# The first expert's input rows are picked by a one-hot product out of SBUF instead of being gathered from DRAM, with the overflow plan and the next index list moved in among its products

## The reference, cut to what matters

```python
def hier_moe(h, p):
    ...
    combine = jnp.einsum('nk,nke->ne', w2, jax.nn.one_hot(eid, N_EXPERTS, dtype=jnp.float32))
    for e in range(N_EXPERTS):
        he = jax.nn.silu(tok @ p['w_exp_gate'][e]) * (tok @ p['w_exp_up'][e])
        y = y + combine[:, e:e + 1] * (he @ p['w_exp_down'][e]).astype(jnp.float32)
```

## Time and profile before

| | |
|---|---|
| median of 3 runs | 1083.66 us (1080.24 to 1084.55) |
| profiled execution, its own time | 1078.97 us |
| its span, first to last instruction | 1077.1 us |
| TensorE busy | 86% of the span |
| DMA, mean over the span | 273 GB/s |
| DMA, 600 to 620 us | 424 GB/s |

### The profile page before, as it was taken

How to read it: one execution, slowest core, us unless ns; L and a number is a source line. 1 busy time by engine, 2 the same in 40 slices (tenths; PEclk the granted TensorE clock), 3 DMA queues, 4 the chain that set the end, 5 groups by cost and what they waited for, 6 DMA issues and landing times.

```text
span 1077.1 us, 14439 instructions
## 1 busy us (share of the span) xinstructions
PE 930.1 (86%) x5814; PEld 625.3 (58%) x5826; DVE 365.8 (34%) x754; ACT 321.5 (30%) x504; POOL 329.3 (31%) x276
## 2 busy tenths in 40 slices
PE   3788999998998989999988999999988888889840
PEld 3677989896897978988653443344333333333310
DVE  4300145845231213858951221212221212112118
ACT  1473343342786858634221000000000000001102
POOL 7544467772234233552010111111111111112112
PEclk9998999999899999999989999999999999999975
DMA  9825534456467692367486999999999999999831
GB/s 325 257 79 103 114 97 78 103 133 169 154 183 216 175 266 101 128 241 290 184 367 249 407 424 425 426 425 426 424 425 427 426 425 426 426 423 425 349 145 56
DMA packets 60821, 294.13 MB, mean 273 GB/s; under 512 B 7525, under 2 KB 9165, under 8 KB 48162
## 3 DMA queue, kind: packets, MB, share of 16 engines
q1 hardware_dynamic: 49296, 272.68, 68.6%
q0 software_dynamic: 6560, 11.47, 3.1%
q10 hardware_dynamic: 4914, 9.28, 2.4%
HBM read 290.23 MB, written 14.68 MB: 283 GB/s over the span
## 4 chain that ended last, share of the span: by engine, by line
PE 46%; DMA 35%; DVE 9%; ACT 5%; issue 4%; POOL 1%; SPq 0%; POOLq 0%; ACTq 0%
DMA ring<-in_w_exp_up 21%; PE bank L1428 13%; DMA ring<-in_w_in 7%; PE bank L1080 5%; PE bank L1451 5%; PE bank L1082 5%; PE bank L1081 5%; DMA cond_slot<-in_w_cond 2%; PE bank L1031 1%; DMA ring<-in_w_branch_a 1%; DMA expert_inputs<-hf 1%; DMA ring<-in_w_cond 1%; PE bank L1418 1%; DVE hf L1941 1%; PE bank L1136 1%
## 5 line engine op out<-in xcount | busy, mean ns | idle before, releaser
L538 POOL TENSOR_TENSOR w_lo<-ring,w_hi 128x1024 fp32r<-128x1024 f32 x80 | 191.9, 2413 | 197.2 <-ACT w_hi L757 197.2
L1428 PE MATMUL bank<-ring,hf 128*64 128x512 f32 x1024 | 229.5, 601 | 17.9 <-DMA ring<-in_w_exp_up 17.0
L1080 PE MATMUL bank<-h_hi,w_hi 128*128 128x320 f32 x576 | 186.1, 323 | 18.0 <-POOL w_lo L538 7.9
L1082 PE MATMUL bank<-h_hi,w_lo 128*128 128x320 f32 x576 | 181.0, 314 | 0.0
L1428 PEld LDWEIGHTS bank<-ring,hf 128*64 128x64 f32 x1024 | 79.6, 139 | 164.3 <-issue 156.4
L1451 PE MATMUL bank<-ring,he 128*64 128x512 f32 x512 | 129.9, 654 | 0.7 <-DVE he L1945 0.5
L1080 PEld LDWEIGHTS bank<-h_hi,w_hi 128*128 128x128 f32 x576 | 111.1, 193 | 23.5 <-ACT va L698 5.4
L1081 PE MATMUL bank<-h_lo,w_hi 128*128 128x320 f32 x384 | 120.4, 314 | 0.0
L1082 PEld LDWEIGHTS bank<-h_hi,w_lo 128*128 128x128 f32 x576 | 110.9, 192 | 0.0
L594 POOL DMA_INDIRECT xrow<-expert_inputs,sidx x32 | 32.8, 1024 | 250.8 <-DVE sidx L1931 230.8
L1941 DVE TENSOR_TENSOR hf<-hf,bank 64x512 f32<-64x512 f32 x32 | 22.1, 690 | 230.2 <-ACT hf L939 230.2
(11 more groups left out here) (376 smaller groups left out, 1276.8 us busy)
## 6 DMA issues: line engine op xcount, KB each, us to landing
ring<-in_w_exp_up SPq DMA_DIRECT2D x32, 2048.0 KB, 34.2
ring<-in_w_exp_down SPq DMA_DIRECT2D x32, 2048.0 KB, 33.5
ring<-in_w_exp_gate SPq DMA_DIRECT2D x32, 2048.0 KB, 29.5
ring<-in_w_in SPq DMA_DIRECT2D x16, 2048.0 KB, 14.0
cond_slot<-in_w_cond SPq DMA_DIRECT2D x9, 2048.0 KB, 11.7
ring<-in_w_cond SPq DMA_DIRECT2D x3, 2048.0 KB, 17.7
ring<-in_w_branch_b SPq DMA_DIRECT2D x2, 2048.0 KB, 7.9
ring<-in_w_branch_a SPq DMA_DIRECT2D x2, 2048.0 KB, 10.8
```

What stands on the lines that cost most here:

```text
L538: pool.tensor_tensor(w_lo[slot][:, :, c], raw[:, :, c], w_hi[:, :, c].bitcast(F32), ALU.subtract)\
L1080: mm(b, hi[:, k, c], x_hi[:, k, :], start=(k == 0), stop=False)
L1082: last = mm(b, lo[:, k, c], x_hi[:, k, :], start=False, stop=(k == KT - 1))
L1428: last = mm(bank[1][64 * q:64 * q + 64, :], xg[:, k % 4, k // 4, :], ring[s + q][:, k * FF:k * FF + FF], start=(k == 0), stop=(k == KT - 1 ...
```

## The change

Expert 0 no longer takes its rows from DRAM. `first_rows` multiplies the token rows in `hf` (stationary, 128 of every fourth column at a time) with the first 64 columns of `onehot` (moving): for each of 2 halves `c` and 4 quarters `q`, three matmuls over the token tiles. VectorE copies the halves out of banks 2 and 0 into `xg_first`, which lies in `gf_rows`; the hidden rows of expert 0 lie there too (`gs_first`). The gather of expert 0 goes, and so do the 16 idle products and the four transposes ahead of `gate_up(0)`. `gate_up(0)` is cut in two halves, with `index(1)` and one product of the plan between them; the other three products of the plan and `index(2)` follow it. On ScalarE `silu(0)` and `rows_out(0)` now stand ahead of the wait for `hf_out`. On VectorE the end of the plan and `one_hots(2)` stand ahead of `gated(0)`.

```diff
+        xg_first = gf_rows[:, 0, 0:CB].rearrange("p (q c s) -> p q c s", q=4, c=2)
+        gs_first = gf_rows[:, 0, CB:CB + FF]
...
             pool.wait_ge(S["hf_out"], 48)
-            gather(0, 0, 0, False)
             gather(1, 1, 1, False)
...
+            silu(0, gs_first)
+            rows_out(0, 0, None)
             act.wait_ge(S["hf_out"], 48)
-            for e in range(3):
+            for e in range(1, 3):
                 step(e, e, None)
...
+            def first_rows():
+
+                pe.wait_ge(S["hb_ready"], 6)
+                pe.wait_ge(S["onehot_ready"], 1)
+                for c, (b, done) in enumerate(((bank[2], "xg_half"), (bank[0], "xg_t"))):
+                    for q in range(4):
+                        for t in range(3):
+                            m = TR[t]
+                            last = mm(b[:, q * SLOTS:(q + 1) * SLOTS], hf[0:m, t, c * CB + q:c * CB + CB:4],
+                                      onehot[0:m, t, 0:SLOTS], start=(t == 0), stop=(t == 2))
+                    last.then_inc(S[done], 1)
...
             idle_products(bank[3], 4)
+            first_rows()
             index(0)
...
-            index(1)
-            pe.wait_ge(S["flag_ready"], 1)
-            mm(bank[4][:, 0:1], tri_strict[:, :], flags[:, 0:1], start=True, stop=True).then_inc(S["xr_ps"], 1)
...
+            pe.wait_ge(S["half_ready"], 1)
+            gate_up(0, 0, use_0, xg_first, range(KT // 2))
+            index(1)
+            pe.wait_ge(S["flag_ready"], 1)
+            mm(bank[4][:, 0:1], tri_strict[:, :], flags[:, 0:1], start=True, stop=True).then_inc(S["xr_ps"], 1)
+            gate_up(0, 0, use_0, xg_first, range(KT // 2, KT))
             pe.wait_ge(S["pick_ready"], 1)
...
-            idle_products(bank[3], 16)
-            turn_rows(0, 0, 16)
-            step(0, 0, lambda s: expert_use(s, 0), 1, 16)
+            index(2)
+            turn_hidden(0, gs_first)
+            turn_rows(1, 1, 16)
+            down(0, 0, use_0)
...
+            dve.wait_ge(S["xg_half"], 1)
+            V.tensor_copy(xg_first[:, :, 0, :], bank[2][:, 0:4 * SLOTS].rearrange("p (q s) -> p q s", q=4))\
+                .then_inc(S["half_ready"], 1)
+            dve.wait_ge(S["xg_t"], 1)
+            V.tensor_copy(xg_first[:, :, 1, :], bank[0][:, 0:4 * SLOTS].rearrange("p (q s) -> p q s", q=4))\
+                .then_inc(S["xg_ready"], 1)
             indexed(0, 0)
...
-            gathered(0)
-            step(0, 2)
+            one_hots(2, 2, None)
+            gated(0, gs_first)
+            indexed(2, 2)
+            turned(0)
+            gathered(1)
```

More of the change, by code:

```diff
@@ L323, in build @@
             flag_ready xr_ps pick_ready plan_ps plan_ready gfr_in gfr_ps gf_ready onehot_ready
-            xg_t xg_ready gu_ps gs_ready hrow_ready he_t he_ready down_ps ys_ready scattered0
+            xg_half half_ready xg_t xg_ready gu_ps gs_ready hrow_ready he_t he_ready down_ps ys_ready scattered0
             scattered1 scattered2 index_ps weighted summed_pool gated_pool comb_in0 comb_in1 comb_in2 vcol_ready
@@ L935, in _, with silu @@
             X.activation(r1[:, 5, :], r1[:, 4, :], ACT.Exp).then_inc(S["ex_out"], 1)
-            def silu(n):
+            def silu(n, gs=gs):
                 act.wait_ge(S["gu_ps"], n + 1)
@@ L1399, in _ @@
             idle_products(bank[3], 4)
+            first_rows()
             index(0)
             pe.wait_ge(S["rep_in"], 1)
-            pe.wait_ge(S["hb_ready"], 6)
             for t in range(3):
@@ L1406, in _ @@
             last.then_inc(S["count_ps"], 1)
-            index(1)
-            pe.wait_ge(S["flag_ready"], 1)
-            mm(bank[4][:, 0:1], tri_strict[:, :], flags[:, 0:1], start=True, stop=True).then_inc(S["xr_ps"], 1)
             def turn_rows(n, b, uses):
-                pe.wait_ge(S[f"gathered{b}"], uses)
+                pe.wait_ge(S[f"gathered{b}"], uses - 16 if b == 0 else uses)
                 if not isinstance(n, int):
@@ L1419, in turn_rows, with gate_up @@
                 last.then_inc(S["xg_t"], 1)
-            def gate_up(n, s, turn):
-                pe.wait_ge(S["xg_ready"], n + 1)
+            def gate_up(n, s, turn, xg=xg, ks=range(KT)):
+                if ks[-1] == KT - 1:
+                    pe.wait_ge(S["xg_ready"], n + 1)
                 pe.wait_ge(chunk_in[s], turn(s))
                 pe.wait_ge(chunk_in[s + 1], turn(s + 1))
-                for k in range(KT):
+                for k in ks:
                     for q in range(2):
@@ L1430, in gate_up, with turn_hidden @@
                                   skip_group_check=True)
-                last.then_inc(S["gu_ps"], 1)
-            def turn_hidden(n):
+                if ks[-1] == KT - 1:
+                    last.then_inc(S["gu_ps"], 1)
+            def turn_hidden(n, gs=gs):
                 pe.wait_ge(S["hrow_ready"], n + 1)
@@ L1462, in step @@
                 down(e, s, use)
+            use_0 = lambda s: expert_use(s, 0)
+            pe.wait_ge(S["half_ready"], 1)
[4 more added lines that the diff above has]
+            gate_up(0, 0, use_0, xg_first, range(KT // 2, KT))
             pe.wait_ge(S["pick_ready"], 1)
@@ L1937, in gathered, with gated @@
                 V.tensor_copy(xg[:, :, :, :].rearrange("p q c s -> p (q c s)"), bank[2][:, :]).then_inc(S["xg_ready"], 1)
-            def gated(n):
+            def gated(n, gs=gs):
                 dve.wait_ge(S["gs_ready"], n + 1)
```

## The result

The changed kernel takes 1091.45 us in the median of 20 runs, the kernel before 1083.46 us in 20 runs beside them. The ratio is 1.0073, 95% interval 1.0052 to 1.0094: 0.7% slower, where 6.1 us less were forecast. The times of one kernel lie 12 to 14 us apart, and one execution of the kernel before took 3600.32 us, which its median does not feel.

The account below looks back on a forecast made before the run. The weight stream's restart after a DMA hole, held back by `gate_up(0)`, was taken as the bound. Issue 6.6 us earlier, less 0.5 us, gives 6.1 us: 1083.66 to 1077.5 us, range 1074 to 1085.

Parts of the forecast that it names:

- What bounds the kernel: Expert stage: its end is set by when the stream of weight transfers begins and by the holes in it.
- the unit price of `first_rows`: TensorE, expert 0's one-hot product: 48 recorded instructions at 0.12 us each, 5.8 us, ending at 558.7 us.
- the bound above: Upper limit on the price of a `first_rows` instruction: 0.17 us, from `xrow`'s four strided transposes; 8.2 us in all.
- The start at 552.90 us: `first_rows` starts on TensorE when expert 0's one-hot list is there, at 552.90 us, where `index(0)` started before.
- The plan, `gated(0)` and the gather of expert 1: Around `gate_up(0)`: 0.5 us lost through VectorE's work; expert 1's gather issued at 563.1 us, with 6 us to spare.
- Strided loads at the dearer price: Rival: `first_rows` takes 8.2 us, gain 3.7 us, 1080 us; chance 0.12.
- The lower level during `first_rows`: Rival: TensorE's clock falls to 0.50, `first_rows` ends at 563.8 us, the gain is gone, 1084.5 us; chance 0.16.
- its sign: What would show the lower clock level: granted clock of 0.50 between 554 and 568 us with `first_rows` over 8 us.
- The slower outcome: Rival: lower clock level from 553.66 us until past `gate_up(0)`, which ends 7.4 us later; 1091 us; chance 0.05.

Follow-up runs that it names:

- e2: Changed kernel with the stationary operand of `first_rows` reading 128 neighbouring columns of `hf` instead of every fourth; ratio 1.0027 to the kernel before, `first_rows` 10.1 us.
- e3: Changed kernel with 12 idle products among the matmuls of `first_rows` and 7 instead of 4 ahead; ratio 1.0084 to the kernel before, `first_rows` 16.8 us.
- e1: Changed kernel again, unedited, for a second profile; ratio 1.0059 to the kernel before, `first_rows` 14.3 us.
- e6: Changed kernel with `first_rows` reading neighbouring columns and its token tiles outermost; ratio 0.9988 to the kernel before, `first_rows` 6.0 us.
- e8: Kernel before again, unedited, for a second profile; ratio 1.0008 to the kernel before.
- e10: Kernel before without the two groups of idle products (8 and 6) in the router's stage; ratio 1.0026 to the kernel before.
- e11: Changed kernel with swapped one-hot operands, without the router's stage's two groups of idle products; ratio 0.9954 to the kernel before.
- e4: Changed kernel with swapped operands in `first_rows`: `onehot` stationary, `hf` moving, then transposes and copies; ratio 0.9928 to the kernel before, `first_rows` 2.9 us.
- e5: Changed kernel with the two inner loops of `first_rows` swapped, token tiles outermost, stride kept; ratio 1.0052 to the kernel before, `first_rows` 12.0 us.

## Why the prediction was wrong

- **What bounds the kernel: right.** From the first expert issue to the end it is 500.7 to 504.4 us in all profiles but one (e2, 506.0, for which no cause was sought), over a range of 19 us in the issue itself.
- **The step that failed: the unit price of `first_rows`.** "The moving side does not matter between them, so I take 0.12: 5.8 us", with 0.17 as the bound above. It measured 0.295 us and 14.2 us. Two things went into it that the two neighbouring rows did not have: a stationary operand of a float32 matmul read with a stride of four elements, and token tiles of 128, 128 and 64 rows in turn. In whole products: 14.2 us with both, 12.0 with the stride alone, 6.0 with neither; 10.1 with the switches alone, half of it at the lower level. All but the first 1 to 2 us of the 14.2 ran at the lower level, but that is not needed for them: with the stride a record costs 0.25 us at the upper level too, which makes 12 us for 48 (an estimate from 8 records of the changed kernel; the first 18 of e3 were no cheaper). Nor is the stride needed at the lower level, at which e2 paid 0.25 us without it. Either one alone spoils the price, and the forecast had neither. The bound of 0.17 came from strided transposes, which are spaced 0.12 us in steady state; it showed that a strided read can be cheap, and was no bound for another kind of instruction.
- **What follows at the lower level, left out of the sum.** The forecast ran everything at the upper level. In e1 `index(0)` cost 1.53 us for 0.9 and the first half of the products 6.42 for 3.5, together 3.5 us more. In e6 the same fall followed a `first_rows` that ran as forecast, and ate 1.8 us.
- The two together explain e1: forecast 15.1 us from list to issue, + 8.5 + 3.5 = 27.1, measured 27.3.
- **The start at 552.90 us: that of one execution.** It is the list's time with the router's stage at the upper level. Over the twelve profiles that kept the stage's idle products the list is 2.0 us later on average, measured from the norm. In the kernel before, the issue moved by 0.6 us when the list moved by 1.5 (e8), as it hangs on the landing of `hf`; in the changed kernel it moved by 3.7 us when the list moved by 5.0 (e1 against the first profile), and in the four builds with swapped operands it lies 14.1 us behind the list every time. By these profiles the change makes the router's stage count, which the forecast did not price. Whether the times show it too is open (e10, e11).
- **The plan, `gated(0)` and the gather of expert 1: right in size.** `down(0)`'s issue came 9.2 us after the first for 9.5 forecast, the fourth 16.2 for 16.5; expert 1's rows never made TensorE wait, although their gather was issued at 585.06 us, behind `index(1)` and far from the 563.1 us that the forecast had. It had overlooked that wait. The wait costs nothing: the gather is issued 2.9 us ahead of the first issue of the stream here and in e4, where the stream is early, and TensorE does not wait there either.
- **The rivals.** "Strided loads at the dearer price" was the right place with a third of the size. The lower level during `first_rows` had 0.16, with 0.24 us a record and 10.9 us in all; its sign, 0.50 with `first_rows` over 8 us, came, and the level fell within `first_rows` in both profiles of the changed kernel, in e2, in e3 and in e5. So, by these profiles, the fall was likelier than 0.16; the rival lacked the switches and the stride. The slower outcome was given 0.05, with 1091 us, and tied to 580 us as the point from which it decides; the issue came 5.5 to 9.2 us later than before (norm to issue), on that side of it. That 1091 is close to the 1091.45 measured is in part luck: the rival had `first_rows` 3.3 us too short, and the second half of the products at the lower level, where it ran at the upper one (3.65 us).
- The Trainium skill's rule (TensorE: Matmul & The Clock Gate, section "LDWEIGHTS (loading the stationary operand)"), that a load costs its columns divided by 1.2 whatever its rows, which gave 107 ns, comes near the distance of records in e6 (44 in 5 us of the upper level, 0.114 us each). It fails for the strided operand (0.25 us at the upper level) and, without a stride, at the lower level (0.25 us in e2, switches included); there the measured numbers stand.

## What to carry to other kernels

A one-hot gather has two forms. Make the one-hot the stationary operand and stream the rows: it loads little, streams 512 columns at a time, and took 2.9 us here where the other form took 14.2. Four transposes and two copies come on top, and it still paid. Before costing a new matmul by a neighbour's row, compare the stride and the partition count of the stationary operand as well as its shape. And after a stretch of loads with little streaming, cost the next products at the lower clock level too: 5.0 to 6.4 us for 3.65 in the six profiles of this kind. And where a forecast starts from a time read in one profile, ask how that time scatters, and whether the new kernel follows it where the old one did not.

## What the runs showed of the hardware

- A float32 matmul's load of 128 stationary columns takes 190 ns with neighbouring columns and 322 ns with every fourth at the upper clock level; at the lower it takes 321 and 324. With the stride the price of a record did not change with the clock (22 in 6 us at 0.50, 8 in 2 us at 0.99); without it, it did (12 in 3 us at 0.50, 21 in 3 us at 1.00). The strided loads of `xrow`'s transposes take 212 ns, those of the norm's transposes, without a stride, 140 (kernel before, from 532.6 us, upper level):

```profile
L1418 PEld LDWEIGHTS bank<-ident,xrow x128: 195/212/227, 565.9 to 1016.7; 128*128 128x128 f32 x128
```

- Four of `xrow`'s transposes with their loads fit in 0.77 us. Why the stride hurts the matmul so much more was not tried.
- Alternating 128-row and 64-row stationary tiles cost 2.2 us over 48 records with the stride. This is the difference of two profiles, e5 and the changed kernel's.
- The granted clock fell to 0.50 during `first_rows` in the five profiles in which it took 10 us or more, and 2 us behind it in e6, with 0.12 us a record; TensorE had run without a gap from the start of `first_rows` to the fall. In the four profiles with swapped operands it stayed at 1.00 from `first_rows` to the end of `gate_up(0)`. No run separates what in the 48 records brings the fall.
